# Latent attention: one 512-column product per chunk of values over high and low probabilities side by side, and a VectorE addition of the two halves of the bank

## The reference, cut to what matters

```python
sc = (jnp.einsum('bqhd,bkhd->bhqk', qn_i, kn)
      + jnp.einsum('bqhr,bkr->bhqk', qr_i, kr)).astype(jnp.float32) * scale
a = jax.nn.softmax(sc, axis=-1).astype(v.dtype)
return jnp.einsum('bhqk,bkhd->bqhd', a, v)
```

## Time and profile before

| | |
|---|---|
| median of 3 runs | 1870.07 us (1866.65 to 1872.04) |
| profiled execution, its own time | 1868.86 us |
| its span, first to last instruction | 1867.1 us |
| PE busy | 1829.6 us (98%), weight loads 1556.9 us |
| DVE, ACT, POOL busy | 1310.4 us, 801.6 us, 823.0 us |
| the attention stage in this span | from about 1300 to 1583 us |

### The profile page before, as it was taken

How to read it: one execution, slowest core, us unless ns; L and a number is a source line. 1 busy time by engine, 2 the same in 40 slices (tenths; PEclk the granted TensorE clock), 3 DMA queues, 4 the chain that set the end, 5 groups by cost and what they waited for, 6 DMA issues and landing times. The chain is left out here.

```text
span 1867.1 us, 27184 instructions
## 1 busy us (share of the span) xinstructions
PE 1829.6 (98%) x9736; PEld 1556.9 (83%) x9736; DVE 1310.4 (70%) x2151; ACT 801.6 (43%) x1581; POOL 823.0 (44%) x568
## 2 busy tenths in 40 slices
PE   6999999999999999999999999999999999999999
PEld 5788888888799888878888888887898898888887
DVE  3598999826688425632679957666777777778886
ACT  6211212211488432211254544432788787445432
POOL 2231233222488563375645341213887983444211
PEclk9999999999999999999999999999999999999999
DMA  5122555443487556565433353594446459658744
GB/s 206 46 68 96 193 160 177 166 149 125 128 285 241 178 189 222 179 209 186 156 111 119 122 168 91 191 355 154 143 159 226 157 176 376 201 177 292 248 147 141
DMA packets 160108, 331.94 MB, mean 178 GB/s; under 512 B 32690, under 2 KB 66226, under 8 KB 159987
## 3 DMA queue, kind: packets, MB, share of 16 engines
q1 hardware_dynamic: 159986, 330.36, 52.6%
HBM read 207.63 MB, written 122.68 MB: 177 GB/s over the span
## 5 line engine op out<-in xcount | busy, mean ns | idle before, releaser
L191 POOL TENSOR_TENSOR w_lo_part<-w_raw,w_hi_part 128x1024 fp32r<-128x1024 f32 x56 | 137.7, 2467 | 338.3 <-ACT w_hi_part L183 338.2
L615 DVE SCALAR_TENSOR_TENSOR ie_ps<-ie_u,ie_wconv,ie_ps 128x1024 f32<-128x1024 f32 x240 | 225.2, 1012 | 0.0
L3492 PE MATMUL og_ps<-w_hi_part,bl_ring 128*128 128x512 f32 x672 | 217.7, 394 | 1.0 <-DVE bl_ring L3025 1.0
L246 PE MATMUL ie_ps<-rows_hi,w_hi_part 128*128 128x512 f32 x384 | 150.8, 393 | 0.0
L246 PE MATMUL ie_ps<-rows_hi,w_lo_part 128*128 128x512 f32 x384 | 149.8, 390 | 0.0
L3492 PEld LDWEIGHTS og_ps<-w_hi_part,bl_ring 128*128 128x128 f32 x672 | 127.0, 189 | 27.1 <-DVE bl_ring L3025 1.1
L246 PE MATMUL ie_ps<-rows_lo,w_hi_part 128*128 128x512 f32 x384 | 149.7, 390 | 0.0
L2913 DVE TENSOR_TENSOR mla_pt_lo<-mla_ps_t,mla_pt_hi 128x512 fp32r<-128x512 f32 x160 | 108.9, 686 | 33.5 <-ACT mla_pt_hi L2882 32.5
L3492 PE MATMUL og_ps<-w_lo_part,bl_ring 128*128 128x512 f32 x336 | 131.5, 391 | 0.0
L2882 ACT CAST mla_pt_hi<-mla_ps_t 128x512 fp32r<-128x512 f32 x160 | 94.1, 592 | 53.5 <-PE mla_ps_t L2833 49.7
L2906 DVE TENSOR_REDUCE mla_min<-mla_ps_s 128x1 f32<-128x1024 f32 (+1 forms) x96 | 100.0, 1042 | 21.9 <-PE mla_ps_s L2823 20.7
(11 more groups left out here) (359 smaller groups left out, 5174.5 us busy)
## 6 DMA issues: line engine op xcount, KB each, us to landing
w_raw<-wall SPq DMA_DIRECT2D x62, 512.0 KB, 4.8
w_hi_part<-weight_blocks SPq DMA_DIRECT2D x28, 512.0 KB, 4.8
w_lo_part<-weight_blocks SPq DMA_DIRECT2D x28, 512.0 KB, 5.8
weight_blocks<-w_hi_part SPq DMA_DIRECT2D x26, 512.0 KB, 6.6
w_raw_tiles<-wall SPq DMA_DIRECT2D x16, 512.0 KB, 5.2
odd_sums<-w_raw_tiles SPq DMA_DIRECT2D x8, 1024.0 KB, 4.4
w_raw<-odd_sums SPq DMA_DIRECT2D x16, 512.0 KB, 4.2
w_flat<-wall SPq DMA_DIRECT2D x16, 512.0 KB, 8.8
```

What stands on the lines that cost most here:

```text
L191: pool.tensor_tensor(g.W[1][:, pair % 2, off:off + QCOLS], g.raw[:, n % 2, :], g.W[0][:, pair % 2, off:off + QCOLS].bitcast(F32), ALU.subt ...
L246: mm = pe.matmul(psum[:, u % banks], w_at(g, name, a, k * HALF + c * P, P), g.XT[m][:, k, b * 512:(b + 1) * 512], start=i == 0, stop=i == ...
L615: dve.scalar_tensor_tensor(out, ubuf[:, cc, at.start + s:at.stop + s], wconv[:, cc, s:s + 1], out, ALU.mult, ALU.add).then_inc(taps, 1)
L3492: mm = pe.matmul(ps[:, N % 4], bl.part(a, N)[:, k], wb.at(N // HT, m, k), start=k + a + m == 0, stop=k == 3 and a == 1)
```

## The change

High and low probabilities move into one tile `mla_pt` whose layout puts the 256 high and the 256 low columns of a chunk next to each other. `weigh` makes one product of 512 columns for a chunk where it made two of 256, with one weight load where there were two; the high sum stands in columns 0 to 255 of the bank and the low sum in 256 to 511. ACT copies the low half into `mla_pv` and signals the new semaphore `halved`; a new DVE instruction, `dve_add`, adds the high half from the bank to it and signals `copied`. It stands in odd steps behind `lo`.

```diff
@@ CREDITS
-              "copied": 1, "back": 2, "inverted": 0, "normed": 1, "prepped": 1}
+              "copied": 1, "halved": 0, "back": 2, "inverted": 0, "normed": 1, "prepped": 1}
@@ attention_tail
-        act.copy(pv_sb[:, q % 2], ps_pv[:, 0:256]).then_inc(pl["copied"], 1)
+        act.copy(pv_sb[:, q % 2], ps_pv[:, 256:512]).then_inc(pl["halved"], 1)
+
+    def dve_add(dve, h6, q):
+        pl.wait(dve, "halved", h6 + q + 1)
+        dve.tensor_tensor(pv_sb[:, q % 2], ps_pv[:, 0:256], pv_sb[:, q % 2], ALU.add).then_inc(pl["copied"], 1)
@@ mla
-        PT = [sb("pt_hi", [P, 2, 8, 256], F32R), sb("pt_lo", [P, 2, 8, 256], F32R)]
+        PT = sb("pt", [P, 2, 8, 2, 256], F32R)
@@ weigh
-                    for part in range(2):
-                        mm = pe.matmul(ps_pv[:, 0:256], ml.V[:, q // NG % 2, k0 + c], PT[part][:, q % 2, c],
-                                       start=c + part == 0, stop=c + part == n)
+                    mm = pe.matmul(ps_pv[:], ml.V[:, q // NG % 2, k0 + c], PT[:, q % 2, c].rearrange("p a k -> p (a k)"),
+                                   start=c == 0, stop=c == n - 1)
@@ scalar engine
-            pl.give(act, "copied", "exped")
+            pl.give(act, "exped")
@@ vector engine
-            pl.give(dve, "lo", "normed")
+            pl.give(dve, "lo", "copied", "normed")
@@ body of the vector engine, behind lo
+                    if step % 2 and live(step - 5):
+                        dve_add(dve, h * NG, (step - 5) // 2)
```

More of the change, by code:

```diff
@@ L781, in dve_norm @@
                           ALU.mult).then_inc(pl["normed"], 1)
-    return act_copy, pe_back, dve_invert, dve_norm
+    return act_copy, dve_add, pe_back, dve_invert, dve_norm
 W0 = (0, 8, 24, 32)
@@ L2758, in mla @@
         g.wait_attn = lambda eng, q: pl.wait(eng, "normed", (HEADS - 1) * NG + q)
-        act_copy, pe_back, dve_invert, dve_norm = attention_tail(g, pl, ps_pv, ps_back, pv_sb, sums, rinv, fold, fold_in)
+        act_copy, dve_add, pe_back, dve_invert, dve_norm = attention_tail(g, pl, ps_pv, ps_back, pv_sb, sums, rinv, fold, fold_in)
         nb = sum(ML_BATCHES)
@@ L2881, in hi @@
                     pl.wait(act, "turned", h * nb + (q + 1))
-                    act.copy(PT[0][:, j // 2 % 2, 4 * b:4 * b + 4, j % 2 * P:(j % 2 + 1) * P],
+                    act.copy(PT[:, j // 2 % 2, 4 * b:4 * b + 4, 0, j % 2 * P:(j % 2 + 1) * P],
                              ps_t[:, q % 2].rearrange("p (c k) -> p c k", k=P)).then_inc(pl["hi"], 1)
@@ L2911, in lo @@
                     pl.wait(dve, "hi", h * nb + (q + 1))
-                    at = lambda part: PT[part][:, j // 2 % 2, 4 * b:4 * b + 4, j % 2 * P:(j % 2 + 1) * P]
+                    at = lambda part: PT[:, j // 2 % 2, 4 * b:4 * b + 4, part, j % 2 * P:(j % 2 + 1) * P]
                     dve.tensor_tensor(at(1), ps_t[:, q % 2].rearrange("p (c k) -> p c k", k=P), at(0).bitcast(F32),
```

## The result

| | before | changed |
|---|---|---|
| median of 20 runs | 1868.61 us (1865.42 to 1872.14) | 1874.28 us (1870.29 to 1877.88) |
| ratio | | 1.0027, 95% interval 1.0020 to 1.0035 |
| span of the profiled execution | 1867.1 us | 1873.0 us |

The account below looks back on a forecast made before the run. PE was taken to bound the kernel, waiting for DVE's low parts at 16 places. Products -1.6, these places +4.5, last head +0.3 and drain +1.2 gave +4.4 us: 1874.5 us against the median 1870.07, range 1869 to 1881.

Parts of the forecast that it names:

- What bounds the kernel: Attention stage: PE sets the time, but stands 0.06 to 0.14 us for DVE's low part at 16 products.
- The gain of the products: Products with the values: 320 pairs become 512-column products, saving 0.005 us a pair, 1.6 us in all, bounds 1.0 to 2.3.
- The price of an addition: New DVE instruction behind the last low part: 0.42 us long, 0.33 us more before PE may start, where not covered.
- The 16 places: Two short-sequence steps per head where PE already waits: 0.28 us each, 4.5 us, bounds 4.0 and 5.3.
- Covered elsewhere: In 29 of the 48 pairs the addition ends before PE needs it and costs nothing; uncovered, up to 0.33 us each.
- The place in the last head: One product, at 1554.22, whose low parts end just ahead of it: the addition costs 0.3 us.
- The drain: Stage's end: two pairs delayed 0.33 us each, last addition ahead of the second-last division; 1.2 us in all.
- The sum: Whole kernel: -1.6 + 4.5 + 0.3 + 1.2 = +4.4 us, 1874.5 us against the median 1870.07, +0.24%; chance 0.64.
- Hidden addition: Rival: DVE's idle time hides the addition, PE loses only part of the drain; -0.6 us, 1869.5; chance 0.13.
- dearer addition: Rival: at 19 exposed places signals and DVE's start add up, 0.55 us each; +9.4 us, 1879.5; chance 0.12.
- DVE as the pace of the stage: Rival: DVE needs its idle time, so all 48 additions show; +14.7 us, 1884.8; chance 0.08.
- weight loads as the saving: Rival: the 320 dropped weight loads ran exposed, 0.08 us each, 26 us less; 1848.9 with the additions; chance 0.03.

Follow-up runs that it names:

- The second run: Changed kernel with the addition left out at the second and third pair of each head (16 of 48): ratio to the kernel before 1.0005, stage 274.67 us.
- Runs 8 to 10: 8: changed kernel, PE's two waits swapped, 1.0024; 9: addition between low parts, drain's division first, waits swapped, 0.9993; 10: as 9, swapped only in loop and drain, 0.9988.
- run 1: Changed kernel without its addition, DVE only passing the signal on: ratio to the kernel before 0.9989, stage 273.13 us.
- run 6: Changed kernel with ACT's copy between its two roundings and DVE's addition between its two low parts: ratio to the kernel before 1.0005, stage 274.43 us.
- run 11: Kernel before, with only PE's two waits swapped in the loop of heads: ratio to the kernel before 0.9984, stage 273.40 us.

## Why the prediction was right

**What bounds the kernel.** Right, and the step on which all rests: the view of waits shows one wait, the distances between PE's starts show 16. The second run took the additions away at just these places and 4.68 of the stage's 4.94 us went.

**The gain of the products, 1.6 us.** Measured 1.67 and 1.63 us, from the products alone. The bounds of 1.0 to 2.3 were too narrow: with every start read to 0.01 us, the two distances allow 0.1 to 3.2. That the middle was met so closely is in part luck. An estimate by the Trainium skill ("TensorE: Matmul & The Clock Gate", Back-to-back issue gap), which gives N/2.4 + 2.5 ns for a product, is 2.5 ns a pair (not 2.6), 0.8 us in all; the rows of the trace were nearer.

**The price of an addition.** 0.41 us long, 0.33 from start to start, as taken from the nearest rows. The 16 places were put at 4.5 us (0.28 each). They cost 12 x 0.25 + 4 x 0.42 = 4.7: in the loop the lower bound, and in the written-out heads 0.09 more than the upper one. Runs 8 to 10 show that the order of the waits makes this difference. Where the wait that ends last stands in the better place with and without the addition, the addition costs 0.33 us in the loop and outside (0.42 to 0.75), and in the worse place the same (0.50 to 0.83, 0.51 to 0.84). The prediction had the possibility of 0.25 but hung it on the shorter waits of the written-out heads, where it did not hold. The middle of the two bounds came out right partly because these errors cancel.

**Covered elsewhere.** Right for one addition in 28 of the 29 pairs, with 0.20 of the 0.53 us of idle time left in a step of the long sequence. The place in the last head cost 0.33 us (0.3 forecast). The 29th, in the first head, was missed: product at 1316.48, 0.61 us behind its transposes instead of 0.36, 0.25 us.

**The drain.** Forecast 1.2 us; last scores to next stage went from 8.67 to 9.98 us, 1.31. The order copy, addition, division, last back product is in the rows above.

**The sum.** Forecast +4.4, stage +4.94 us: +4.7 + 0.33 + 0.25 + 1.3 - 1.65 = +4.93. The median of this series, 1868.61, lies 1.5 us below the one that the forecast was set against, so 1874.28 against 1874.5 is nearer than the mechanism deserves; the ratio, +0.27% against +0.24%, is the fair measure. The measurement with 20 runs turned out finer than the 0.3% named, and tells the small loss from none; the forecast had thought this improbable.

**The rivals.** Hidden addition, dearer addition (0.55 us a place), DVE as the pace of the stage, and weight loads as the saving: none is what happened. For the dearer addition DVE would have had to wait for ACT's copy, which it did once in 48 times. The weight loads are excluded by run 1 as well, since there nothing is left but the saving.

## What to carry to other kernels

Before an instruction is put behind another on a side engine, look at what the bound engine waits for from there, from start to start and not in the list of waits: a hidden wait of 0.06 to 0.14 us meant here that an instruction of 0.33 us added in front of its signal was paid with 0.25 to 0.42 us at each place, while the same work a little earlier, in that engine's own wait, cost nothing at the same 16 places (run 6). Moving it puts off what then stands behind it, as at the one place of the last head. Halving the count of products while the columns stay was worth only the difference of the starts, here 5 ns a pair.

## What the runs showed of the hardware that I had not expected

The order of two waits ahead of the same product is worth 0.07 to 0.09 us, and which order is better differs between the loop and the written-out code. In the loop of heads the wait that ends last should stand second (0.42 against 0.50, 0.75 against 0.83 us, runs 8, 9 and 11). In the written-out heads it should stand first (0.42 against 0.51, 0.75 against 0.84, runs 8 to 10), and the drain's first pair, written out too, agrees (0.70 against 0.78, run 8). A visible difference is that the counts are computed in the loop and constant outside; no run changes that alone, so that it is the reason is not shown, and why the two are opposite is open.

PE's granted clock dipped at the stage's start in some executions, whatever the kernel. These windows are those of the changed kernel, from 1296 to 1310 us (the third number from the right is the granted clock, 1.00 its level of 2.4 GHz and 0.50 that of 1.2; PE busy is the second number):

```profile
1296.00:1302.00 6.00, 3.26 (x16) 2.42 (x15) 5.61 (x8) 1.49 (x3) 0.00 (x0) 1.00 0.34 131
1302.00:1306.00 4.00, 4.00 (x17) 3.39 (x17) 1.97 (x3) 2.11 (x5) 0.00 (x0) 0.64 0.57 166
1306.00:1310.00 4.00, 4.00 (x24) 3.36 (x23) 3.29 (x5) 3.20 (x6) 0.00 (x0) 0.93 1.13 202
```

In the profile before the same windows read 1.00, and in that of run 1 as well, where PE had been busy just as long in the first of them (3.26 us). From the first scores to the first product with the values it was 12.15 us before and 13.70 here; but run 1 (same products) had 12.15, and run 11, whose work there is that of the kernel before, 13.69. So the dip does not follow the change, and this is why the stage was measured from its first product with the values. From 1312 to 1576 us the granted clock is 1.00 in all 13 profiles.
